# Thirty-two gate columns on four column groups, and a new order of work in the linear attention phase

## The reference

```python
low @ w_decay[d] + b_decay[d]          # [tokens, 16] @ [16, 128]
log_a = log_sigmoid(...) / B_GATE_TAU  # B_GATE_TAU = 16
```

## Time and profile before

| | us |
|---|---|
| median of 3 runs | 3420.76 |
| the profiled execution | 3419.75 |
| its span | 3417.9 |
| TensorE (PE) busy | 3252.6 (95%) |
| VectorE (DVE) busy | 1246.8 (36%) |
| ScalarE (ACT) busy | 890.6 (26%) |
| mean granted TensorE clock | 0.97 |

### The profile page before, as it was taken

One profiled execution on the slowest core, in us unless ns is written; L12 is line 12 of the kernel. 1 busy time (PEld: TensorE's weight loads), 2 busy tenths in 40 slices (PEclk: granted clock), 3 DMA queues, 4 the chain that ended last, 5 costly groups with the idle time before them and its releaser, 6 DMA issues. The chain is left out here.

```text
span 3417.9 us, 26806 instructions
## 1 busy us (share of the span) xinstructions
PE 3252.6 (95%) x10208; PEld 1578.3 (46%) x10208; DVE 1246.8 (36%) x1598; ACT 890.6 (26%) x1571; POOL 90.7 (3%) x106
## 2 busy tenths in 40 slices
PE   9998998999999998999999989978997999999997
PEld 4343443444444443444455445554464444444444
DVE  7834763233333333443210047664655011111113
ACT  2111773011111113343100036554312211111111
POOL 0000000000000000000000000030000000000002
PEclk9999999999999999999999999979978999999998
DMA  3114702101111104332321000011002988988874
GB/s 125 49 39 110 229 1 99 42 32 42 37 37 37 37 25 163 143 125 100 86 51 36 0 1 1 2 48 71 21 3 112 358 332 340 343 333 334 332 295 180
DMA packets 101972, 406.07 MB, mean 119 GB/s; under 512 B 7632, under 2 KB 8048, under 8 KB 97136
## 3 DMA queue, kind: packets, MB, share of 16 engines
q1 hardware_dynamic: 90208, 362.22, 29.4%
q0 software_dynamic: 7056, 25.69, 2.0%
q10 hardware_dynamic: 4608, 16.78, 1.2%
HBM read 367.96 MB, written 54.53 MB: 124 GB/s over the span
## 5 line engine op out<-in xcount | busy, mean ns | idle before, releaser
L2551 PE MATMUL ex_up_ps<-big,ex_xT 128*128 128x512 f32 x1024 | 452.7, 595 | 3.0 <-ACT ex_xT L2611 3.0
L1199 PE MATMUL fm_ring<-V,fm_up 128*128 128x512 f32 x704 | 316.6, 592 | 0.0
L1199 PE MATMUL fm_ring<-fm_n,fm_up 128*128 128x512 f32 x704 | 316.5, 592 | 0.0
L1428 PE MATMUL dn_acc<-big,V 128*128 128x512 f32 x704 | 305.4, 596 | 1.6 <-PEq L43 1.6
L2551 PEld LDWEIGHTS ex_up_ps<-big,ex_xT 128*128 128x128 f32 x1024 | 193.1, 191 | 234.2 <-issue 230.8
L1448 PE MATMUL dn_acc<-h,dn_tail 128*128 128x512 f32 x544 | 235.6, 592 | 0.0
L2570 PE MATMUL ex_y_ps<-ex_wd,ex_hT 128*128 128x512 f32 x512 | 227.7, 598 | 6.0 <-DVE ex_hT L2660 6.0
L1428 PEld LDWEIGHTS dn_acc<-big,V 128*128 128x128 f32 x704 | 134.6, 191 | 170.7 <-issue 170.7
L1199 PEld LDWEIGHTS fm_ring<-fm_n,fm_up 128*128 128x128 f32 x704 | 133.8, 190 | 168.4 <-issue 168.4
L1199 PEld LDWEIGHTS fm_ring<-V,fm_up 128*128 128x128 f32 x704 | 133.7, 190 | 167.9 <-issue 167.9
L678 PE MATMUL f_acc<-h,f_w 128*128 128x512 f32 x416 | 182.4, 598 | 0.0
(11 more groups left out here) (442 smaller groups left out, 3859.2 us busy)
## 6 DMA issues: line engine op xcount, KB each, us to landing
big<-in_w_eup SPq DMA_DIRECT2D x32, 4096.0 KB
ex_wd<-in_w_edown SPq DMA_DIRECT2D x32, 2048.0 KB, 13.1
y_dram<-in_cos SPq DMA_DIRECT2D x1, 24576.0 KB, 83.1
fm_up<-in_w_up SPq DMA_DIRECT2D x22, 1028.0 KB, 4.8
dn_tail<-in_w_mod SPq DMA_DIRECT2D x32, 512.0 KB, 7.1
y_dram<-big ACTq DMA_DIRECT2D x32, 512.0 KB, 7.8
V<-in_w_down SPq DMA_DIRECT2D x8, 1408.0 KB, 6.8
dn_tail<-in_w_in SPq DMA_DIRECT2D x17, 512.0 KB, 3.8
```

What stands on the lines that cost most here:

```text
L1199: mm = nc.tensor.matmul(slot(x)[:, a:a + BANK], up[:, i % 2, (2 * k + s) * P:(2 * k + s + 1) * P], n[k][:, a:a + BANK], start=(k == 0), st ...
L1428: mm = nc.tensor.matmul(o[:, x * BANK:(x + 1) * BANK], wd[j % 2][:, k * P:(k + 1) * P], hidden[:, k, x * BANK:(x + 1) * BANK], start=(k == ...
L2551: mm = nc.tensor.matmul(up_ps[:, s, :], xT[:, u, k, :], wu[:, u, k, s * H:(s + 1) * H], start=(k == 0), stop=(k == KD - 1))
```

## The change

1. Tile 7 of the input projection (`LOW`) uses 32 of its 128 weight columns, and its eight matmuls over the contraction go to four column groups of the array in turn: k = 0, 4 to PSUM partitions 0 to 31, k = 1, 5 to 32 to 63, and so on. Each group ends with a partial sum.
2. `w_dec` is laid out four times over the partitions, so that z contracts over all 128 rows and adds the four partial sums. It is loaded in phase "an", as the first of `o2_first`, into a place that is free there.
3. In "go", TensorE's order becomes: z, parts 0 to 3, level 0 with the two halves of part 4 in it, transposes, summands with parts 5 and 6, levels 1 to 7 with half of part 6 + n after each two units, o, half of part 14, token sums, the other half and half of part 15, the spread, the rest of part 15. A half is three matmuls.
4. VectorE runs the scans before `keep(0)`: `add_part(0)`, `sum_up(0)`, `add_part(1)`, `sum_up(1)`, the key arguments, `add_part(2)`, `keep(0)`, key products, `add_part(3)`, `add_part(4)`, `arguments(1)`. Parts 14 and 15 are added in the norm.
5. ScalarE takes one small Sqrt (8 columns) ahead of the norm's roots.

```diff
+    LOW = 7
+                def narrow_or_wide(c, k, o, a, weights, src):
+                    n = src.shape[-1]
+                    if c == LOW:
+                        g = 32 * (k % 4)
+                        return nc.tensor.matmul(o[g:g + 32, a:a + n], weights[:, 0:32], src, start=(k < 4), stop=(k >= 4))
+                    return nc.tensor.matmul(o[:, a:a + n], weights, src, start=(k == 0), stop=(k == KD - 1))
-                        mm = nc.tensor.matmul(o[:, x * BANK:(x + 1) * BANK], wq[:, y % 4, k, :], h[:, k, x * BANK:(x + 1) * BANK],
-                                              start=(k == 0), stop=(k == KD - 1))
+                        mm = narrow_or_wide(c, k, o, x * BANK, wq[:, y % 4, k, :], h[:, k, x * BANK:(x + 1) * BANK])
...
-                sp.dma_start(wd[0:32], w_dec).then_inc(dec_in, 16)
...
-                def part(i):
+                def part(i, halves=(0, 1)):
...
-                        nc.tensor.matmul(z_ps[:, d, a:a + BANK], wd[0:32, d, :], low[0:32, a:a + BANK], start=True, stop=True)
-                    nc.tensor.matmul(z_ps[:, d, T:W], wd[0:32, d, :], low_c[0:32, :], start=True, stop=True).then_inc(z_ready, 1)
-                part(0)
-                part(1)
-                for u in range(4):
-                    unit(0, u)
-                for i in range(2, 7):
+                        nc.tensor.matmul(z_ps[:, d, a:a + BANK], wd[:, d, :], low[:, a:a + BANK], start=True, stop=True)
+                    nc.tensor.matmul(z_ps[:, d, T:W], wd[:, d, :], low_c[:, :], start=True, stop=True).then_inc(z_ready, 1)
+                for i in range(4):
                     part(i)
+                unit(0, 0)
+                unit(0, 1)
+                part(4, (0,))
+                unit(0, 2)
+                unit(0, 3)
+                part(4, (1,))
...
-                        if u == 1:
-                            part(8 + n)
+                        if u % 2:
+                            part(6 + n, (u // 2,))
...
+                part(14, (0,))
                 for i in range(2):
                     pe.wait_ge(squared, i + 1)
...
+                part(14, (1,))
+                part(15, (0,))
                 for i in range(2):
                     pe.wait_ge(widened, i + 1)
...
+                part(15, (1,))
...
+                nc.scalar.activation(decay[:, 0, :], cst["lane"][:, 0:C], ACT.Sqrt)
...
                 add_part(0)
-                keep(0)
-                add_part(1)
-                add_part(2)
                 dve.wait_ge(read, 3)
                 sum_up(0)
+                add_part(1)
                 sum_up(1)
...
-                add_part(3)
-                add_part(4)
-                arguments(1)
+                add_part(2)
+                keep(0)
                 dve.wait_ge(powers, 1)
...
-                add_part(5)
-                add_part(6)
+                add_part(3)
+                add_part(4)
+                arguments(1)
...
+            o2_first = Loads([(w_dec, din["w_dec"], dec_in)] + [(w_o2[u], din["w_out2a"][u].rearrange("p (k n) -> p k n", n=P), w_o2_ready[u]) for u in range(2)])
...
-    d["w_dec"] = dec
+    d["w_dec"] = np.concatenate([dec] * 4, axis=0)
```

More of the change, by code:

```diff
@@ L1463, in _ @@
                         for k in range(KD):
-                            mm = nc.tensor.matmul(acc[:, pos["q", order[y]] % 2, T:T + NCTX], wq[:, y % 4, k, :], nctx[:, k, :],
-                                                  start=(k == 0), stop=(k == KD - 1))
+                            mm = narrow_or_wide(order[y], k, acc[:, pos["q", order[y]] % 2, :], T, wq[:, y % 4, k, :],
+                                                nctx[:, k, :])
                     mm.then_inc(done, 1)
@@ L1709, with gla_and_out @@
 GLA_HALVES = (64, 32, 16, 8, 4, 2, 1)
-def gla_and_out(nc, tag, cst, vecs, din, h, h_dram, gate2, others, w, wb, xb, pr, pc, rows, V):
+def gla_and_out(nc, tag, cst, vecs, din, h, h_dram, gate2, others, w, dec_in, wb, xb, pr, pc, rows, V):
     W = T + NCTX
@@ L1729, in gla_and_out @@
     out, gate = pr[:, 6:8, :], pr[:, 15:17, :]
-    w_dec, b_dec, gain = din["w_dec"], vecs["b_dec"], vecs["gla_g"]
+    b_dec, gain = vecs["b_dec"], vecs["gla_g"]
     n_out = 2 * KD
@@ L1756, in gla_and_out @@
         h_in = [ph.sem(f"h_in{x}") for x in range(KD)]
-        dec_in, masks_in, wb_in = (ph.sem(s) for s in ("dec_in", "masks_in", "wb_in"))
+        masks_in, wb_in = ph.sem("masks_in"), ph.sem("wb_in")
+        ph.sems.append(dec_in)
         z_ready, read, log_ready, step, own = (ph.sem(s) for s in ("z_ready", "read", "log_ready", "step", "own"))
@@ L1880, in _ @@
                     if j in (5, 11):
-                        part(7 + (j == 11))
+                        part(5 + (j == 11))
                 for n in range(1, N + 1):
@@ L2097, in _ @@
                             V_.tensor_tensor(qe[:, d, :], qe[:, d, :], q, ALU.mult).then_inc(qe_ready, 1)
-                        add_part(7)
+                        add_part(5)
                     if j == 11:
                         weigh(1)
-                        add_part(8)
+                        add_part(6)
                 arguments(2)
@@ L2110, in _ @@
                     keep(n - 1)
-                    add_part(7 + n)
+                    add_part(5 + n)
                 keep(N)
-                add_part(8 + N)
+                add_part(6 + N)
                 for i in range(2):
@@ L2124, in _ @@
                         3).broadcast_to([P, TT, 2, 64])).then_inc(widened, 1)
+                add_part(14)
                 for i in range(2):
@@ L2129, in _ @@
                                             op0=ALU.mult, op1=ALU.mult).then_inc(normed, 1)
+                add_part(15)
 def route(nc, tag, cst, vecs, din, h, mixed, wb, big, V, mod, a2, r, h2_dram, wu, u_ready, xb, x_ready):
@@ L2816, in second_block, with experts_block @@
                           scale_q=True, ahead=o2_first)
[L2819 removed]
+def experts_block(nc, din, cst, vecs, h, h_dram, mod, a2, big, pc, vr, V, w_o2, dec_in, y_dram, y_filled, out, stack):
     with ExitStack() as outer:
@@ L2963, in program @@
             w_o2_ready = [nc.alloc_semaphore(f"o2_w_ready{u}") for u in range(4)]
-            o2_first = Loads([(w_o2[u], din["w_out2a"][u].rearrange("p (k n) -> p k n", n=P), w_o2_ready[u]) for u in range(2)])
+            dec_in = nc.alloc_semaphore("dec_in")
+            w_dec = flat[:, 17 * T + 6 * P:18 * T].rearrange("p (d n) -> p d n", d=2)
+            o2_first = Loads([(w_dec, din["w_dec"], dec_in)] + [(w_o2[u], din["w_out2a"][u].rearrange("p (k n) -> p k n", n=P), w_o2_ready[u]) for u in range(2)])
             second_block(nc, din, cst, vecs, h, mod, neg_lam, sub_g[:], pr, pc, v2, vr, o2_first)
-            experts_block(nc, din, cst, vecs, h, h_dram, mod, a2[:], big, pc, vr, V, (w_o2, w_o2_ready), y_dram, y_filled, out, stack)
+            experts_block(nc, din, cst, vecs, h, h_dram, mod, a2[:], big, pc, vr, V, (w_o2, w_o2_ready), dec_in, y_dram, y_filled, out, stack)
 VECS = [("mix_g", KD), ("mem_g", KD), ("ffn_g", KD), ("q_g", 10), ("mk_g", 2),
```

16 lines of the change are left out of this document (9 added, 7 removed).

## The result

The changed kernel takes 3383.51 us (median of 4 runs, 3379.55 to 3390.00), the kernel before beside it 3421.26. The ratio is 0.989, with a 95% interval of 0.9873 to 0.9907. The direction was right and the size was not. The changed kernel's profiled execution took 3383.86, 0.35 above its median.

The account below looks back on a forecast made before the run. TensorE, busy for 95% of the span, was taken as the bound, slowed by clock dips and waits. Terms -12.6 - 21.1 + 0 + 6.5 = -27.2 from 3420.8 gave 3393.5 us; own range 3386 to 3400, wider 3384 to 3405.

Parts of the forecast that it names:

- Tile 7: Input projection: four column groups run at once, 4.6 us instead of 17.2, so -12.6 us.
- Rival (a): Tile 7: only two column groups run at a time, everything else as forecast, 3397.8 us; chance 0.16.
- rival (b): Tile 7: the narrow matmuls don't overlap at all, 3406 us; chance 0.05.
- The start of "go": Front of the linear attention phase: transposes start at 2399.8 and not 2420.9, -21.1 us, bounds -17 and -23.
- I expect the full clock 4 to 6 us after the start: 2.5 us lost: Start of "go": z over 128 rows still begins at a low clock, which costs 2.5 us.
- VectorE's chain: Front of "go": scans run before level 0 is kept; TensorE waits about 2 us for the multiplied keys.
- Summands, levels and norm: Later "go": summands 0; levels 0 (bounds -9 and +11); norm +6.5 us (bounds +4 and +13).
- Rivals (c): Levels and norm give back the front's gain, levels +11 and norm +10, 3408 us; chance 0.09.
- (d): Levels and norm: TensorE stays at 1.2 GHz through both, so the kernel is slower, 3443 us; chance 0.04.
- Everything after is TensorE's stream, so it moves up as a whole: Code after the touched parts: it shifts earlier with them, adding no term to the sum of -27.2 us.
- low end: Bottom of the forecast's wider range, 3384 us: the levels at -9 alone.

Follow-up runs that it names:

- e4: Changed kernel with tile 7 on two column groups of 64 instead of four of 32: 3390.35 us.
- e3: Changed kernel with the decay weights loaded at the start of the linear attention phase again, as its first load: 3386.93 us.
- g_dec_late: Repeat of e3's edit against the changed kernel, in the last batch beside the changed kernel run again: 3392.65 us.
- e8: Changed kernel with the parts in levels 1 to 7 whole again, after the second unit: 3387.75 us.
- e6: Changed kernel with each part in levels 1 to 7 cut 5 : 1 instead of 3 : 3: 3375.86 us.

## Why the prediction was wrong

**Tile 7** was right in mechanism and size: 4.4 us measured, 4.6 forecast. Rival (a), two at a time, is what e4 shows for two groups, 8.7 us, and rival (b) is out. The quoted rule of the Trainium skill ("TensorE: Matmul & The Clock Gate", Part 3), "strict FIFO, no reordering", does not hold for starts here. For column groups this rests on the program's order, which the trace does not list: the kernel calls the matmuls of the four groups one after another, each of them is two instructions, and still the first instructions of all four begin within 0.02 us, and the next four together 0.45 us later. For row groups the trace of the kernel before shows it directly: of the two units that begin at 2490.60 in the earlier trace rows, the last instruction of the first, the one that signals its end, is the 21st to start, though the unit has 16; five instructions of the next unit start before it.

**The start of "go"** is a term that was mis-sized: -24.1 measured, -21.1 forecast. The failed step is "I expect the full clock 4 to 6 us after the start: 2.5 us lost". The clock never fell: the granted clock of the front is 1.00. I had seen the wait for the decay weights only as 1.6 us of time. Without it TensorE stands for 1.46 us only, and the clock had not fallen behind that pause; in e3 and g_dec_late, with the wait put back, the full clock comes 3.1 and 5.3 us after z's start, so the step would have held for a start behind the wait. VectorE's chain came out as worked, only 2 us earlier, since z was: the first scan begins 12.8 us after z's start where 14.7 was forecast, and the transposes come after a wait of 2.06 where about 2 was said.

**Summands, levels and norm** were right as sums, -0.5 and +6.8, and in part by luck. In the levels the new waits and the better clock (0.88 against 0.82) do cancel: TensorE is busy for 7.3 us less (73.08 against 80.34) and stands 5.8 us more. e8 shows the terms apart: without the halves the levels take 89.4. But the forecast had one wait of 3 us in each of levels 3 to 7 and 13.7 us for each level. Levels 3, 4 and 5 take 15.2, 13.6 and 13.6 us, and 6 and 7, without a wait, 9.5 and 8.7; before, the five took 63.6 together, not 5 x 13.5. In the norm two misses cancel. The 3.6 us taken for the 16 transposes at the full clock was read off a row at 1.2 GHz (3.65 in the earlier trace rows); they take 1.8. And the low clock costs more than the 1.5 us allowed: the sums take 4.2 where 3.4 was said and the two halves behind them 7.9 where 5.2 was said. Rivals (c) and (d) did not come.

**The unchanged phases** hold the rest of the miss, and the step that failed is "Everything after is TensorE's stream, so it moves up as a whole". The touched parts account for 30.7 and 30.1 us in the two profiles, 3 more than forecast. The medians differ by 37.7 and 39.9. What is left, 7 to 10 us, is in code that is the same. The profiles show 5.1 and 3.1 of it, the first mostly in differential attention, the second from `route` on; that of the kernel before was also 1.5 faster than its median, and the second of the changed kernel 3.3 slower than the median of its eight. In differential attention the clock is low for 3.4 or 17 us instead of 10, by when it first falls, and that is as far as the cause is shown: why the executions of the changed kernel fare better on average stays open. My range gave this no term: its low end held nothing but the levels at their best, though the kernel's own executions lie as much as 10 us apart (3379.55 to 3390.00). That is why it was too narrow.

## What to carry to other kernels

Float32 matmuls with 32 output columns ran four at a time here when their contraction was split over four column groups; if the consumer is itself a matmul, it adds up the partial sums without an instruction more. A wait at the start of a phase is worth its own length and what the clock loses by it, so load ahead whatever its first matmul needs. And a phase in which TensorE waits often (it is busy for 90% of differential attention) moves by some 5 us from one execution of a kernel to the next: profile the same kernel twice before a difference in untouched code is given to an edit.

## What the runs showed that I had not expected

- Four matmuls with 128 contraction rows and 32 columns each, over 512 float32 tokens, hold the array for no longer than one at full width: 32 of them take 3.46 us from start to the next (1846.51 to 1849.97), 0.108 each, against 0.43.
- A pause of 1.46 us between matmuls over 512 tokens left the clock at 2.4 GHz; one of 3.57 us in the same place (e3) was followed by z's first matmuls at 1.2 GHz. The length alone does not decide: in the levels of e6 a pause of 1.71 us was followed by two units at 1.2 GHz (3.22 us, where 1.72 is their time at the full clock).
- Differential attention takes 216.8 to 221.3 us in identical code, by when the clock first falls in it, and not evenly: 216.8 to 217.0 in nine of eighteen profiles, 217.8 and 218.3 in two, 219.8 to 220.3 in five, 221.3 in two. The changed kernel is in the first group and in the last. Neighbourhood attention, without the wait for the decay weights, takes 109.1 to 114.1.
